# Transformer block with retrieval of experts: 64 late slots, pairs of tokens in the one-hot products, low weight parts by GpSimd

## The reference

```python
h = rms_norm(x, norm_mix_gain); proj = h @ w_in          # q, k, v of two attentions, gates
kc, vc = compress(k_c, ...), compress(v_c, ...)          # gelu(flat @ w1) @ w2, 15 blocks x 2 groups
x = x + merged @ w_out                                   # two attentions, gated
# PEER: 8 heads x 16 of 16384 experts for each token
top_s, pos = top_k(s1 + s2); eidx = ...; g = softmax(top_s)
a = gelu(einsum('cd,ced->ce', x_norm, expert_down[eidx]))     # 128 slots of each token
out = einsum('ce,ced->cd', a * g, expert_up[eidx])
return rms_norm(x + out, norm_final_gain)
```

## Time and profile before

| what | value |
|---|---|
| median of 3 runs | 2262.41 us (2258.6 to 2264.26) |
| the profiled execution | 2256.19 us |
| its span, first to last instruction | 2254.4 us |
| busy time of PE, DVE, ACT, POOL | 1681.9, 1616.9, 836.1, 536.7 us |
| mean granted TensorE clock | 0.843 |
| moved by DMA | 602.96 MB, mean 267 GB/s |

### The profile page before, as it was taken

One profiled execution on the slowest core, in us unless ns is written; L12 is line 12 of the kernel. 1 busy time (PEld: TensorE's weight loads), 2 busy tenths in 40 slices (PEclk: granted clock), 3 DMA queues, 4 the chain that ended last, 5 costly groups with the idle time before them and its releaser, 6 DMA issues.

```text
span 2254.4 us, 24153 instructions
## 1 busy us (share of the span) xinstructions
PE 1681.9 (75%) x9330; PEld 1463.8 (65%) x9330; DVE 1616.9 (72%) x2021; ACT 836.1 (37%) x1192; POOL 536.7 (24%) x340
## 2 busy tenths in 40 slices
PE   5999999999999995001000124389999999999997
PEld 4979977999998895001000123278887888888886
DVE  4424445434455587999999999975488899899864
ACT  3313325433433531000000568864443434434433
POOL 0301200000000004666656658600012111111100
PEclk9999987999999998555555555558999999999999
DMA  6566540455566457998998889903699999999964
GB/s 218 171 193 229 181 131 1 149 177 179 185 224 225 153 165 271 393 362 344 361 367 341 352 352 427 394 0 112 223 351 368 416 387 383 385 387 387 387 216 149
DMA packets 145028, 602.96 MB, mean 267 GB/s; under 512 B 13760, under 2 KB 24768, under 8 KB 88896
## 3 DMA queue, kind: packets, MB, share of 16 engines
q0 software_dynamic: 43776, 318.79, 35.6%
q1 hardware_dynamic: 93712, 280.05, 35.3%
q10 hardware_dynamic: 7472, 3.27, 0.5%
HBM read 599.98 MB, written 2.10 MB: 267 GB/s over the span
## 4 chain that ended last, share of the span: by engine, by line
PE 66%; DVE 25%; POOL 3%; DMA 3%; issue 2%; ACT 1%; ACTq 0%; DVEq 0%
PE psum L560 65%; DVE down_rows L1812 16%; POOL down_rows L1000 3%; DMA late_rows<-in_peer_expert_down_dram,eidx 1%; DMA down_rows<-in_peer_expert_down_dram,eidx 1%; DVE oh L1899 1%; DVE w_lo L1474 1%; DVE onehot L1769 0%; DVE onehot L1766 0%; DVE key L1771 0%; PE psum L769 0%; DVE late_rows L1812 0%; PE psum L575 0%; DVE pos L1724 0%; DVE pos L1717 0%
## 5 line engine op out<-in xcount | busy, mean ns | idle before, releaser
L1000 POOL DMA_INDIRECT down_rows<-in_peer_expert_down_dram,eidx x208 | 395.5, 1902 | 786.0 <-DVE w_lo L1474 599.3
L1474 DVE TENSOR_TENSOR w_lo<-raw,w_hi 128x2048 fp32r<-128x2048 f32 x124 | 286.5, 2310 | 366.7 <-ACT w_hi L1080 366.4
L1812 DVE CUSTOM_DVE_ANT_0 down_rows<-down_rows,xn 128x2048 f32<-128x2048 f32 x208 | 465.1, 2285 | 11.0 <-DMA down_rows<-in_peer_expert_down_dram,eidx 9.2
L560 PE MATMUL psum<-u_hi,c_hi 128*128 128x512 f32 x1024 | 400.2, 391 | 4.3 <-DVE c_lo L1909 2.2
L560 PE MATMUL psum<-u_lo,c_hi 128*128 128x512 f32 x1024 | 399.8, 390 | 0.0
L560 PE MATMUL psum<-u_hi,c_lo 128*128 128x512 f32 x1024 | 399.6, 390 | 0.0
L1080 ACT CAST w_hi<-raw 128x2048 fp32r<-128x2048 f32 x124 | 236.1, 1904 | 437.9 <-PE psum L560 404.5
L1905 DVE TENSOR_TENSOR u_lo<-u_raw,u_hi 128x2048 fp32r<-128x2048 f32 x128 | 293.5, 2293 | 91.1 <-ACT u_hi L1374 90.7
L560 PE MATMUL psum<-act_hi,w_hi 128*128 128x256 f32 x1088 | 309.9, 285 | 2.4 <-DVE w_lo L1474 2.4
L560 PE MATMUL psum<-act_lo,w_hi 128*128 128x256 f32 x1088 | 308.6, 284 | 0.0
L560 PE MATMUL psum<-act_hi,w_lo 128*128 128x256 f32 x1088 | 308.5, 284 | 0.0
(11 more groups left out here) (268 smaller groups left out, 2338.3 us busy)
## 6 DMA issues: line engine op xcount, KB each, us to landing
u_raw<-in_peer_expert_up_dram SPq DMA_DIRECT2D x128, 1024.0 KB, 7.3
raw<-in_w_in_dram SPq DMA_DIRECT2D x76, 1024.0 KB, 5.0
raw<-in_w_out_dram SPq DMA_DIRECT2D x16, 1024.0 KB, 5.1
raw<-in_peer_w_query_dram SPq DMA_DIRECT2D x16, 1024.0 KB, 5.0
raw<-in_w_up_nsa_dram SPq DMA_DIRECT2D x8, 1024.0 KB, 5.1
raw<-in_w_up_fox_dram SPq DMA_DIRECT2D x8, 1024.0 KB, 5.0
raw<-in_k_cmp_w_dram SPq DMA_DIRECT2D x4, 1024.0 KB, 5.3
raw<-in_v_cmp_w_dram SPq DMA_DIRECT2D x4, 1024.0 KB, 5.6
```

The lines of the kernel that those rows point to most:

```text
L560: return nc.tensor.matmul(*a, skip_group_check=True, **k)
L1000: nc.gpsimd.indirect_dma_start(rows[:], None, table, bass.IndirectOffsetOnAxis(ap=eidx[:, half, slot:slot + 1], axis=0)).then_inc(landed, 16)
L1474: tt(w_lo[:, p % 2], raw[:, p], f32(w_hi[:, p % 2]), ALU.subtract).then_inc(lo_done, 1)
L1812: return V.tensor_tensor_reduce(out=rows[:], in0=rows[:], in1=xn[:, half, :], scale=1.0, scalar=0.0, op0=ALU.mult, op1=ALU.add, accum_out= ...
```

## The change

The late slots of half 1 become 64 (LATE_H = 4), its dense slots 64. The late rows get a fifth buffer at 0 KB, free when the spreading is over; some values that lived there move to keep. Eight late operations stand in chunks 1, 3, ..., 15, the others from chunk 17 on, with two in every twelfth chunk. GpSimd makes c_lo (c_low) in place of VectorE, and issues the gathers behind it. The second half's one-hots are made for two tokens at a time, one on partitions 0 to 63 and one on 64 to 127: 16 batches of four pairs, all one-hots by VectorE, eight products of 64 rows each and two copies for a batch; four products of W stand before each batch (IDLE). The first half's batches are placed over 56 dots instead of 78. At the start TensorE does 40 products of ones; ScalarE's six small transfers are issued by GpSimd; the first high part stands ahead of the wait for cols. The compress products go in turn to four strips of 32 output partitions, and a product with fold adds the strips up.

```diff
-LATE_H = 5
+LATE_H = 4
 DENSE = (SLOTS, LATE_H * TOPK)
 LATE = SLOTS - DENSE[1]
 NG = (DENSE[0] + DENSE[1]) // GS
 SPREAD_G = SLOTS // GS
 NUM1_AT = 16
 DVE_ROWS = 1
-LATE_C0 = 18
-LATE_RING = 4
+LATE_AT = (10, 74, 18, 82, 0)
+LATE_FREE = (16, 16, 32, 32, 0)
+LATE_EARLY = (1, 3, 5, 7, 9, 11, 13, 15)
+LATE_C0 = 17
+LATE_TWICE = 12
 LATE_A = 32
+IDLE = 4
 BT = 4
 NB = P // BT
+PAIRS = P // 2
+NB1 = PAIRS // BT
...
+        late_step = list(LATE_EARLY)
+        for i in range(LATE_C0, NKEYS):
+            late_step += [i, i] if (i - LATE_C0) % LATE_TWICE == LATE_TWICE - 1 else [i]
+        late_step = late_step[:2 * LATE]
+        assert len(late_step) == 2 * LATE
+        late_slot, late_turn, late_before = [], [], []
+        last_op = {}
+        for j, i in enumerate(late_step):
+            free = [r for r in range(len(LATE_AT)) if LATE_FREE[r] < i or LATE_FREE[r] == 0]
+            r = min(free, key=lambda r: last_op.get(r, -1))
+            late_slot.append(r)
+            late_before.append(last_op.get(r))
+            late_turn.append(late_slot.count(r))
+            last_op[r] = j
+
+        def late_after(j):
+
+            return LATE_FREE[late_slot[j]] - 1 if late_before[j] is None else late_step[late_before[j]]
...
+            pe.wait_ge(const_done, 1)
+            for _ in range(40):
+                mm(psum[:, 6, 0:P], ones[:], ones[:], start=True, stop=True)
...
-                                last = mm(psum[0:GROUPS * NCMP, 6 + kv, 0:CMP_HID],
-                                          flat[:, kv, 8 * p + r, :, :].rearrange("p g n -> p (g n)"), w1[:, r, :],
-                                          start=p == 0 and r == 0, stop=p == PIECES - 1 and r == 7)
+                                at_ = CMP_ROWS * (r % 4)
+                                last = mm(psum[at_:at_ + CMP_ROWS, 6 + kv, 0:CMP_HID], flat[:, kv, 8 * p + r, :], w1[:, r, :],
+                                          start=p == 0 and r < 4, stop=p == PIECES - 1 and r >= 4)
                             last.then_inc(cmp_used, 1)
                 if b == 5:
+                    pe.wait_ge(hidp_done, 1)
+                    for kv in range(2):
+                        last = mm(psum[0:GROUPS * NCMP, 6 + kv, CMP_HID:2 * CMP_HID],
+                                  const("fold")[:, 0:GROUPS * NCMP], hidp[:, kv, :], start=True, stop=True)
+                    last.then_inc(hid_ps, 1)
...
+            def numbers_T_twice():
+                pe.wait_ge(num_done, 2)
+                pe.wait_ge(numT_done, 1)
+                for a in range(2):
+                    for l in range(2):
+                        ins = mm(psum[a * PAIRS:(a + 1) * PAIRS, 0, l * P:(l + 1) * P], key12[:, l, 0:DENSE[1]], ident,
+                                 start=True, stop=True)
+                ins.then_inc(num_ps, 1)
+
+            def weights_T_twice():
+                pe.wait_ge(w_done, 2)
+                pe.wait_ge(wT_done, 1)
+                for a in range(2):
+                    ins = mm(psum[a * PAIRS:(a + 1) * PAIRS, 1, 0:P], gw[1].rearrange("p h s -> p (h s)")[:, 0:DENSE[1]], ident,
+                             start=True, stop=True)
+                ins.then_inc(w_ps, 1)
...
+            def spread_pairs(b):
+
+                bank, par = 2 * (b % 2), b % 2
+                pe.wait_ge(W_out, NB + (b - 1 if b >= 2 else 0))
+                for _ in range(IDLE):
+                    mm(psum[:, bank, 0:P], W[:, 1, 0, :], W[:, 1, 0, :], start=True, stop=True)
+                pe.wait_ge(oh_ready, NB + b + 1)
+                for q in range(BT):
+                    for a in range(2):
+                        rows_ = slice(a * PAIRS, (a + 1) * PAIRS)
+                        ins = mm(psum[:, bank + a, q * P:(q + 1) * P], oh[rows_, 0, par, q, :], oh[rows_, 1, par, q, :],
+                                 start=True, stop=True)
+                ins.then_inc(W_ps, 1)
...
+            weights_T_twice()
+            pe.wait_ge(numT_done, 2)
+            pe.wait_ge(wT_done, 2)
+            for b in range(NB1):
+                spread_pairs(b)
...
+            def ld(dst, src):
+                pool.dma_start(dst, src).then_inc(late_loaded, 16)
+
+            pool.wait_ge(raw_loaded[1], 16)
+            ld(bias32[:, 0:NGATE], nsa_gate_bias.partition_broadcast(P))
+            ld(bias32[:, NGATE:32], fox_forget_bias.partition_broadcast(P))
+            ld(gf_raw[:, :, 0:NGATE], w_in_v[:, :, G_N:G_N + NGATE])
+            ld(gf_raw[:, :, NGATE:32], w_in_v[:, :, F_F:F_F + FOX_H])
+            ld(w2[:, 0], k_cmp_w2[0].rearrange("(c p) d -> p c d", p=P))
+            ld(w2[:, 1], v_cmp_w2[0].rearrange("(c p) d -> p c d", p=P))
...
+            def c_low(i):
+
+                pool.wait_ge(c_hi_done, i + 1)
+                if i >= 2:
+                    pool.wait_ge(chunk_used, i - 1)
+                nc.gpsimd.tensor_tensor(c_lo[i % 2][:], W[:, :, i, :], f32(c_hi[:, i % 2]), ALU.subtract).then_inc(c_lo_done, 1)
+
+            def late_gather(j):
+
+                r = late_slot[j]
+                if late_before[j] is not None:
+                    pool.wait_ge(late_used, late_before[j] + 1)
+                elif LATE_FREE[r] == 0:
+                    pool.wait_ge(W_ps, NB + NB1)
+                else:
                     pool.wait_ge(c_lo_done, LATE_FREE[r])
-                else:
-                    pool.wait_ge(late_used, late_before(j) + 1)
                 gather(late_rows[r], (peer_expert_down if j < LATE else peer_expert_up)[0], 1, DENSE[1] + j % LATE,
                        late_in[r])
+
+            pool.wait_ge(eidx_done, HALVES * PEER_H // 2)
+            late_gather(0)
+            issued = 1
+            for i in range(NKEYS):
+                c_low(i)
+                while issued < 2 * LATE and i >= late_after(issued) + (late_before[issued] is not None):
+                    late_gather(issued)
+                    issued += 1
+            for j in range(issued, 2 * LATE):
+                late_gather(j)
...
             nc.scalar.copy(cols[:], psum[:, 7, 0:P]).then_inc(cols_done, 1)
+            hi_piece(0, 0)
             act.wait_ge(cols_done, 1)
-
-            def hi_piece(b, p):
...
+                    nc.scalar.copy(hidp[:], psum[:, 6:8, 0:CMP_HID]).then_inc(hidp_done, 1)
+                if b == 6:
+                    act.wait_ge(hid_ps, 1)
                     for kv in range(2):
-                        nc.scalar.copy(hid[:, kv, :], psum[0:GROUPS * NCMP, 6 + kv, 0:CMP_HID]).then_inc(ga_done, 1)
-                if b == 6:
+                        nc.scalar.copy(hid[:, kv, :], psum[0:GROUPS * NCMP, 6 + kv, CMP_HID:2 * CMP_HID]).then_inc(ga_done, 1)
...
+            def spread_pairs_out(b):
+                act.wait_ge(W_ps, NB + b + 1)
+                bank = 2 * (b % 2)
+                for a in range(2):
+                    t = a * PAIRS + BT * b
+                    ins = nc.scalar.copy(W[:, 0, :, t:t + BT].rearrange("p i t -> p t i"),
+                                         psum[:, bank + a, :].rearrange("p (t i) -> p t i", i=NKEYS))
+                ins.then_inc(W_out, 1)
...
+            def one_hots_pairs(b):
+
+                par, p0 = b % 2, BT * b
+                dve.wait_ge(W_ps, NB + b - 1)
+                n2 = numT[:, 1, 1, p0:p0 + BT].unsqueeze(2).to_broadcast([P, BT, NKEYS])
+                tt(oh[:, 0, par], iota128[:].unsqueeze(1).to_broadcast([P, BT, NKEYS]), n2, ALU.is_equal)
                 for q in range(BT):
-                    ins = ts(oh[0:k, 1, par, q, :], iota128[0:k], numT[0:k, 1, 0, bass.ds(t0 + q, 1)],
-                             wT[0:k, bass.ds(t0 + q, 1)], ALU.is_equal, ALU.mult)
+                    ins = ts(oh[:, 1, par, q, :], iota128[:], numT[:, 1, 0, p0 + q:p0 + q + 1], wT[:, p0 + q:p0 + q + 1],
+                             ALU.is_equal, ALU.mult)
                 ins.then_inc(oh_ready, 1)
...
+            def late_op(j):
+                if j < LATE:
+                    late_dot(j)
+                else:
+                    late_add(j)
+                if j == LATE_A:
+                    late_inner(0, LATE_A)
+                if j == LATE_A + 3:
+                    late_weights(1, 0, LATE_A)
+                if j == LATE:
+                    late_inner(LATE_A, LATE)
+                if j == LATE + 3:
+                    late_weights(2, LATE_A, LATE)
...
-                        t, n_ = GS * (G - SPREAD_G) + q - 2, GS * (NG - SPREAD_G) - 2
-                        for b in range(NB * max(t, 0) // n_, NB * max(t + 1, 0) // n_):
+                        t, n_ = GS * (G - SPREAD_G) + q - 2, GS * (NG - SPREAD_G) - 8
+                        for b in range(min(NB, NB * max(t, 0) // n_), min(NB, NB * max(t + 1, 0) // n_)):
...
+            for b in range(NB1):
+                one_hots_pairs(b)
+            dve.wait_ge(W_ps, NB + NB1)
             for i in range(1, NKEYS):
-                c_low(i)
                 u_low(i)
-                j = i - LATE_C0
-                if 0 <= j < LATE:
```

(36 more changed lines are left out.)

217 lines of the change are left out of this document (95 added, 122 removed).

## The result

The changed kernel takes 2198.6 us (median of 4 runs, 2198.5 to 2201.1) against 2260.5 before (4 runs, 2258.6 to 2264.3): ratio 0.9727, 95% interval [0.9715, 0.9739]. The prediction was 2193, range 2180 to 2250. So the ledger of the two traces (a table of where the time went, stage by stage) shows 55.1 us where the medians show 61.9.

The account below looks back on a forecast made before the run. Bounds: TensorE in projections, second spreading (setting the pace at half clock) and up stage; VectorE in the dense stage. -8 - 6 - 35.5 - 26 + 5 + 1.5 = -69: 2187 us profiled, 2193 median; range 2180 to 2250.

Parts of the forecast that it names:

- Start: Before the first w_hi: without ScalarE's issue of small transfers w_hi starts at 15.5, gain 8 us, bounds 10 and -8.
- Compress: Compress stage: four strips run at once, 6.9 us instead of 27.6, then w1's pieces set the pace at 20; gain 6.
- Dense stage: Dense stage: 16 dots of 2.21 us leave VectorE's path, 35.4 us gained, bounds 33 and 39.
- 20 us of cover are left: Dense stage: ScalarE's 32 one-hot batches, 159 us, fit within VectorE's shortened stage of 181 us.
- Second spreading: Second spreading: paired batches at 2.4 GHz, 2.3 us each, stage 43 us; gain 26, bounds gain 31 and loss 27.
- (2.6 + 2.06)/2: Second spreading: idle products and pairs, 2.6, then ScalarE's copies, 2.06, in a loop two batches deep: 2.3 us a batch.
- Up stage: Up stage: single late operations free, nine doubled chunks cost 9.5 us, early ones 2.3; 708 against 702.9, +5.
- The ramp: Up stage: the ramp's part of 6.6 us of ramp and stalls goes too, if the clock is up.
- (a): Second spreading: pairs run at low clock; total 2219 if they overlap, 2248 if not; chance 0.23.
- (b): Start: GpSimd's small transfers come late, 16 us of stall, total 2209; chance 0.10.
- (c): Up stage: shared-port lock paces it, GpSimd's c_lo exceeding the 1.02 us gap; 1.3 us gives 2224, 1.75 gives 2274; chance 0.14.
- (d): Up stage: DMA bounds chunks 17 to 127 at 363 GB/s, 667 us against 604, total 2253; chance 0.06.

Follow-up runs that it names:

- The second run on the start: The six small transfers issued by ScalarE again, none by GpSimd, against the changed kernel: 2208.7 us, ratio 0.9774 to the kernel before.
- The exponential's run: ScalarE's exponential for the last pair of heads moved behind batch 15 instead of 12, against the changed kernel: 2199.3 us, ratio 0.9726 to the kernel before.

## Why the prediction was right, and by which steps

The total came out because the terms were right in kind. Two of them, compress and dots, were too large by 12 us in all; the errors of the others had both signs and left 2 us. In the ledger the sum is -55 against -69, so the mechanism was priced 14 us too high. The median was off by 5.6 us only, since 8.7 us of the error lie in how the two profiled executions stand to their medians (6.2 below the one that I took, 2.5 above). That part is luck.

**Start.** Predicted 8 gained, w_hi at 15.5; it came at 13.70. The bound of 15 took the median landing of raw, 10.7 us, for the first piece; issued at 4.33, that one was there by 13.70, 9.4 us later at most. The ones end at 12.8, not at 15 or 20. The second run on the start shows the cause to be the issue on ScalarE alone. The ones don't matter. One microsecond went back at once: the clock was low for the first 3 us of main products, against 1.3 before.

**Compress.** Predicted -6, got -1.2. The step that failed is not the strips' overlap (3.66 us for half of the products are 7.3 for all, against the 6.9 taken) but its end: the stage was priced by the 8 MB of w1, without the first piece of block 5, which queues behind them, and without w_hi and w_lo of that piece, 4.4 us from 159.47 to 163.84; and nothing was put in for the clock. The product that started at 177.5 before starts at 163.8, 13.7 us earlier counting the 8.7 of the start, so 5.0 were gained there, 1.0 less than predicted. The other 3.8 were lost behind it: about 3 of them are half clock to 170.0, and the rest is open.

**Dense stage.** Predicted 35.4; the dots 160 and on gave 28.0. "20 us of cover are left" was the wrong step: busy time of ScalarE in a stage of 181 us counts as cover only if ScalarE can run ahead, and just where it could have, it stood 10.1 us for the last exponential, with a wait of 8.5 us for TensorE at batch 16 behind that. Moving both returned 7.7 us, moving the first alone 1.5. With both moved the gain is 35.7, so the price of the 16 dots themselves was right.

**Second spreading.** Predicted 43 us for the stage, measured 44.0, the gain 29.2 instead of 26 since the stage before was counted as 69 from a later mark. The clock was at 2.4 GHz as taken, a batch 2.18 us (2.3). But the mechanism behind (2.6 + 2.06)/2 was not the one at work: TensorE alone was the bound, 1.09 + 1.09. The idle products that I priced as part of the pace were the pace.

The Trainium skill (TensorEngine Tiling (Array Packing), Key Properties) says that tiles load and multiply in parallel. The trace agrees for alternating halves, 1.09 us for eight; in sequence it is 1.64 and not 2.18, so the alternating order gives 0.55. It agrees for the four strips too, 3.66 us for 13.8.

**Up stage.** Predicted 9.5 for nine doubled chunks, measured 9 x 1.2 = 11; single operations cost nothing, as said, and neither did the early ones, for which 2.3 stood in the sum (in the one profile with waits for rows they cost some 6). The ramp didn't go, the step that failed here: TensorE stands 3.3 us ahead of the first product, and the clock was at half for the first 6 us of it, which is 3 us.

The Trainium skill (SBUF — State Buffer, SBUF: two separate sides) calls the pair of ports an exclusive lock. The trace agrees: c_lo that comes during a dot ends 0.6 to 0.7 us behind it, and a dot that comes during c_lo takes 2.82 us instead of 2.28. The runs with c_lo on VectorE show that this makes the move worthless.

**End.** +0.7 instead of +1.5: final_row landed in 4.5 us.

**Rivals.** (a) cold pairs: not in this kernel, but the order of the products alone brings them, 73.7 us for the stage. (b) no: GpSimd's two issues of gf_raw took 2.35 us together, not 15 each. (c) no, though its sign came: GpSimd's c_lo is recorded at 1.42, above the 1.0 that I had called wrong and the 1.02 us of gap. At the rival's price that would be 44 us. The sign was badly chosen, since the record starts while c_lo still waits for the dot. What counts in the gap is the part behind the dot, 0.6 to 0.7 us, as the forecast had it. (d) no: the windows of 100 us from 1600 to 2100 show 389 to 404 GB/s with TensorE 98 to 99% busy.

## What to carry to other kernels

Cover isn't busy time subtracted from a stage: before dots are taken out from under another engine's work, list the waits in that engine's own program, and move all gates of a chain, since removing the first only shows the second. Faster products in front of a full DMA queue end in waiting, and the price continues behind it in a lowered clock. Products added to hold the clock up must be tried against none: in the second spreading the real work did it, and the added ones were the bound. A duration in a profile can hold a wait: read an operation that shares something with another engine from the other's end.

## What the runs showed of the hardware

- The granted clock rose after two batches of alternating 64-row products and idle ones, and also without any idle ones; with the same products in sequence, TensorE busy throughout, it stayed at 1.2 GHz for 50 us.
- A product of 64 rows in sequence with others of the same rows and bank is not half of one of 128: 1.64 us for eight against 1.09 for four; alternating halves, and banks with them, make it 1.09.
- Products of 32 output columns in four strips of one bank overlap: 32 of them in 3.66 us, where 64 one behind the other took 27.6.
- GpSimd's c_lo (0.74 us alone) beside a dot of VectorE waits for the dot's end and ends 0.6 to 0.7 us behind it; a dot that starts during c_lo takes 2.82 us instead of 2.28.
- In profiles of the same code up to dot 32, the spells at 1.2 GHz in compress and attention came in two lengths (20.5 and 41.0 us, or 17.1 and 37.5), and the time from the first compress product to dot 32 with them: 818.5 us in the changed kernel's profile, 816.0 in that with c_lo on VectorE. The exponential's run, 2195.5 and 2195.8 in two runs and 2199.3 to 2199.7 in three, shows two such levels in its times; that they are the same thing was not tried.
- The two strided transfers of gf_raw (192 and 64 KB) cost 8.5 to 8.8 us to issue on ScalarE and 2.35 on GpSimd.
